# Moving one operand buffer of a float32 two-block transformer kernel by 64 bytes

## The reference

```python
# first block: attention without softmax, then a squared-ReLU MLP
a = rms_norm(x, norm_mix);  q, k, v = split(a @ w_qkv)            # 2048 -> 3 x 2048
A = exp(log_sigmoid(z) + sum of -softplus(z) over later keys)      # z = q k / sqrt(128), masked
h = x + (A @ v) @ w_o
h = h + square(relu(rms_norm(h, norm_mlp) @ w1)) @ w2              # 2048 -> 8192 -> 2048
x = rms_norm(h, final_norm)
# second block: 16 meta tokens are put in front of the 256
hn = rms_norm(concat(meta, x), norm_mix_g)
u, gb, gc, v, ga, gbr = split(hn @ w_in)                           # 2048 -> 6 x 2048
y_a = (trailing means of u over 2, 4, 8, 16 tokens, minus u) @ pool_w * pool_scale
y_b = (gb * causal_conv3(gc * v)) @ conv_out_w
h = x + (sigmoid(ga + b) * y_a + sigmoid(gbr + b) * y_b) @ w_o
h = h + (silu(rms_norm(h) @ w_gate) * (rms_norm(h) @ w_up)) @ w_down   # 2048 -> 5632 -> 2048
out = rms_norm(h, norm_final_g)[the 256 tokens]
```

## Time and profile before

| what | value |
|---|---|
| median of 3 runs | 2618.42 us (2618.08 to 2618.51) |
| the profiled execution | 2618.09 us |
| its span (first to last instruction) | 2616.4 us, granted TensorE clock 0.999 |
| PE busy | 2606.8 us, 16309 products |
| PEld busy | 2351.2 us, 16309 loads |
| DVE, ACT, POOL busy | 1648.6, 1213.5, 142.4 us |
| chain that ended last | PE 99% |
| HBM | 185 GB/s over the span |

### The profile page before, as it was taken

The page is one execution under the profiler, slowest core; times in us unless marked ns, Lnnn a source line. Parts: engine busy times, 40 slices in busy tenths (PEclk is TensorE's granted clock), DMA queues, the critical chain, the costliest instruction groups (busy, mean ns, idle before and its releaser), DMA issues.

```text
span 2616.4 us, 41094 instructions
## 1 busy us (share of the span) xinstructions
PE 2606.8 (100%) x16309; PEld 2351.2 (90%) x16309; DVE 1648.6 (63%) x1406; ACT 1213.5 (46%) x1189; POOL 142.4 (5%) x87
## 2 busy tenths in 40 slices
PE   9999999999999999999999999999999999999998
PEld 9999998888888888899899988888888888888887
DVE  6577666656556556787654776566756555655665
ACT  5455544444444444544533344444544444444444
POOL 0001100000000000000200620000000000000001
PEclk9999999999999999999999999999999999999999
DMA  7554555565565565555555555555555555555563
GB/s 261 183 171 161 163 176 181 190 192 183 188 192 185 186 191 189 181 179 191 182 190 177 180 190 192 184 186 193 187 185 191 191 183 189 192 183 186 193 202 120
DMA packets 243953, 485.24 MB, mean 185 GB/s; under 512 B 7728, under 2 KB 8944, under 8 KB 243696
## 3 DMA queue, kind: packets, MB, share of 16 engines
q1 hardware_dynamic: 243520, 483.12, 56.6%
q10 hardware_dynamic: 320, 0.53, 0.1%
HBM read 481.53 MB, written 2.10 MB: 185 GB/s over the span
## 4 chain that ended last, share of the span: by engine, by line
PE 99%; DVE 0%; DMA 0%; ACT 0%; issue 0%; POOL 0%; SPq 0%; DVEq 0%; ACTq 0%; POOLq 0%
PE ps L1324 46%; PE ps L1330 24%; PE ps L1344 14%; PE ps L1352 7%; PE ps L1312 4%; PE ps L1318 2%; PE ps L1454 0%; PE ps L1366 0%; PE ps L1400 0%; DMA raw<-in_sb_w_qkv_dram 0%; PE ps L1388 0%; PE ps L1459 0%; PE ps L1437 0%; PE ps L1391 0%; DVE wlo L761 0%
## 5 line engine op out<-in xcount | busy, mean ns | idle before, releaser
L761 DVE TENSOR_TENSOR wlo<-raw,whi 128x1024 fp32r<-128x1024 f32 x900 | 1135.3, 1270 | 915.5 <-ACT whi L554 912.6
L554 ACT ACTIVATE whi<-raw 128x1024 fp32r<-128x1024 f32 x900 | 952.4, 1061 | 1314.3 <-PE ps L1330 982.2
L1324 PE MATMUL ps<-b_buf,whi 128*128 128x512 f32 x2688 | 673.3, 392 | 0.0
L1324 PE MATMUL ps<-a_buf,whi 128*128 128x512 f32 x2560 | 645.7, 394 | 0.0
L1324 PEld LDWEIGHTS ps<-b_buf,whi 128*128 128x128 f32 x2688 | 483.5, 189 | 86.5
L1324 PEld LDWEIGHTS ps<-a_buf,whi 128*128 128x128 f32 x2560 | 459.7, 188 | 84.9
L1330 PEld LDWEIGHTS ps<-b_buf,wlo 128*128 128x128 f32 x2688 | 366.7, 190 | 26.2
L1330 PE MATMUL ps<-b_buf,wlo 128*128 128x256 f32 x2688 | 374.8, 282 | 0.0
L1330 PEld LDWEIGHTS ps<-a_buf,wlo 128*128 128x128 f32 x2560 | 346.9, 188 | 27.1
L1330 PE MATMUL ps<-a_buf,wlo 128*128 128x256 f32 x2560 | 354.3, 281 | 0.0
L1344 PE MATMUL ps<-a_buf,whi 128*128 128x258 f32 (+4 forms) x2560 | 330.9, 282 | 0.1
(11 more groups left out here) (190 smaller groups left out, 1052.8 us busy)
## 6 DMA issues: line engine op xcount, KB each, us to landing
raw<-in_mlp_w_dram SPq DMA_DIRECT2D x128, 1024.0 KB, 5.1
raw<-in_w_in_dram SPq DMA_DIRECT2D x96, 1024.0 KB, 5.0
raw<-in_w_gate_up_dram SPq DMA_DIRECT2D x88, 1024.0 KB, 5.0
raw<-in_sb_w_qkv_dram SPq DMA_DIRECT2D x44, 1024.0 KB, 5.1
raw<-in_w_down_dram SPq DMA_DIRECT2D x44, 1024.0 KB, 5.1
raw<-in_sb_w_o_dram SPq DMA_DIRECT2D x16, 1024.0 KB, 5.1
raw<-in_conv_out_w_dram SPq DMA_DIRECT2D x16, 1024.0 KB, 5.0
raw<-in_w_o_dram SPq DMA_DIRECT2D x16, 1024.0 KB, 5.1
```

Source lines behind the costliest of these rows:

```text
L554: act.activation(whi[:, unit_of(n, u)], raw[:, n % RAW, u * UK:(u + 1) * UK, :], ACT.Copy).then_inc(w_hi, 1)
L761: dve.tensor_tensor(wlo[:, s], raw[:, n % RAW, u * UK:(u + 1) * UK, :], cast(whi[:, s]), ALU.subtract).then_inc(w_lo, 1)
L1324: pe.matmul(ps[:, 4 * half + j, :].rearrange("p (a n) -> p a n", a=2), whi[:, s, kt, j * P:(j + 1) * P], buf[:, :, x, tok], start=first an ...
```

## The change

Before `b_buf` is placed, the offset goes up by 64 bytes. `b_buf` and all that follows up to `ms` (`h`, `full`, `U`, `S1`, `S2`, `acc`, `rr`, `rr1`, `ms`, and `x_sq`, which shares `b_buf`'s place) start 64 bytes later. `msum` has no place of its own any more: the sum goes to the first 16 columns of `rr`. Since `msum` took 64 bytes, `vec` and all behind it stay where they were. No instruction is added, removed or moved.

```diff
         a_buf, _ = place("a_buf", [P, 2, NT, TW], F32R)
+        top[0] += 64
         b_buf, b_off = place("b_buf", [P, 2, NT, T], F32R)
@@
-        msum, _ = place("msum", [P, M])
+        msum = rr[:, 0:M]
@@
-                dve.tensor_reduce(msum[:], U[:, 1, 0:NT * M].rearrange("p (t n) -> p n t", n=M), mybir.AxisListType.X,
+                dve.tensor_reduce(msum, U[:, 1, 0:NT * M].rearrange("p (t n) -> p n t", n=M), mybir.AxisListType.X,
@@
-                    pe.matmul(ps[:, 6, 0:M], ones[:], msum[:], start=True, stop=True, skip_group_check=True)
+                    pe.matmul(ps[:, 6, 0:M], ones[:], msum, start=True, stop=True, skip_group_check=True)
```

## The result

The changed kernel took 2604.09 us (median of 5 runs, 2603.82 to 2604.91) against 2618.22 us before: ratio 0.9946, 95% interval 0.9936 to 0.9957, 14.1 us less. The prediction was 2613.9 us with a range of 2607 to 2620.

What follows compares the result with a forecast made beforehand. The prediction took the spacing of TensorE's products, which have no idle time ahead, to bound the kernel. Its terms, -3.5 - 2.3 + 1.3 = -4.5 us, gave a predicted median of 2613.9 us, range 2607 to 2620.

Steps and rivals of the forecast that it cites:

- What bounds the kernel: Whole kernel: products have no idle time ahead, so only their start-to-start spacing can change time beyond a few tenths of a microsecond.
- The 256s with `wlo`: 2688 products of 256 columns on `b_buf`: 119.1 to 117.8 ns each, -3.5 us, bounds -11.0 and +2.4 us.
- The 512s: 2688 products of 512 columns on `b_buf`: 230.0 to 230.5 ns each, +1.3 us, bounds -6.7 and +13.4 us.
- The narrow products: 960 products on `b_buf`, 640 with `whi` and 320 with `wlo`: 120.0 to 117.6 ns each, -2.3 us.
- Attention: 80 products of L1366 and L1376 that read `b_buf`: taken as nothing, at most 0.2 us either way.
- the other operands: Operands of VectorE, ScalarE and GpSimd that move by 64 bytes: taken at zero.
- `msum`: The sum placed in `rr`: no instruction or wait more, zero, not above 0.1 us either way.
- no effect: Product spacing on `b_buf`: the remainder does not matter or 64 bytes aren't enough to leave it; 2618.4 us, 26%.
- The slower one: 512-column products on `b_buf` lose their settled 227.5 ns rhythm and go to 235 ns; +7.6 us, 2626 us, 10%.
- The conflict removed: Weight load and stream collide at the shared remainder; a constant offset gives 227.5 and 115 ns, -22.5 us, 2596 us, 14%.
- The bounds: Whole kernel: the terms' bounds together, -22.5 us (2596) and +15.8 us (2634).

## Why the prediction was wrong

*What bounds the kernel*: right. The gain is in product spacing alone, and no idle time appeared beyond the 0.3 us of one wait.

*The 256s with `wlo`*: this step failed, and is the larger part of the miss. It took `a_buf`'s mean of 117.8 ns for `b_buf` at 64 bytes, -3.5 us; measured 115.7 ns, -9.1 us. The nearest row, the k tile of `a_buf` that stands at 64 bytes, would not have saved it. Its 0.46 us for four products comes from two rounded starts; by the unrounded starts of the same trace they take 0.468 us, 117.0 ns each. That the bound of 115 ns lies near the 115.7 measured was luck. In `a_buf` the distance changes every four products, while in `b_buf` it is constant, and there every second unit runs at 113 ns throughout. Nor is `a_buf`'s mean that of the constant places it walks through: with TensorE alone those give 115.7, 118.5, 114.0 and 119.1 ns, 116.8 on average, and `a_buf`'s rows 118.1. The prediction saw a settled rhythm in the 512s of before and did not ask which one the new place would have for the 256s.

*The 512s*: this term failed as well, by 4.5 us: taken as +1.3 us, measured -3.2 us (229.0 ns). The 227.5 ns rhythm of the second half was lost, as feared, and the halves of a unit are equal, 0.91 to 0.92 us. But the new rhythm serves all eight alike: 226, 229 and 232 ns in turn, by the starts of the trace.

*The narrow products*: -2.3 us taken, -1.8 us measured, right in size.

*Attention, the other operands, `msum`*: at nothing, and nothing it was (everything but `b_buf` moved: 0.9999).

*The rivals*: no effect, 26%, is out. The slower one, 10%, is not what happened at 64 bytes, yet it is real at 128, where the kernel is 4.4 us slower (232.8 ns per 512). The conflict removed, 14%, comes nearest, and my argument against it, that `a_buf` off the remainder is no better, was the error of the whole: a mix of distances says little on one constant distance. The argument also counted modulo 512 bytes; the period is 256, so `a_buf` is off the remainder in three of four k tiles and not in seven of eight. But the mechanism of this rival is not shown either: of the 15 other distances tried in steps of 16 bytes, 12 have slower units than the shared remainder, so it is not a conflict that ends when that is left. The bounds, 2596 to 2634, held the time; the range, cut at the middle of that rival, did not.

What stays open is why the distance matters inside TensorE, and what decides between two rhythms at one place. The first was not tried below whole products, nor without the weight loads. Of the second the traces show that narrow units on `b_buf` change their rhythm only where other products or a wait come between them, never inside an unbroken run; nothing here predicts which one they take.

## What to carry to other kernels

Where products follow one another without idle time, sweep the byte distance between weights and moving operand modulo 256 bytes with TensorE alone: 16 places of 8 units each take under 0.4 ms of one run. The paired units tried in the full kernel came within 0.1% of that price. The narrow ones on `b_buf` did so at 0 and 128 bytes alone, since at 64 and 192 they can take either of two rhythms 4% apart. Don't take a buffer whose rows walk through several distances as the price of a constant one. "Not the same remainder" is no rule: 64 bytes gained 14.1 us, 192 gained 11.8, 128 lost 4.4.

## What the runs showed of the hardware

- The distance of operand and weights counts modulo 256 bytes, and moves a unit of 16 products between 2.757 and 2.833 us (2.8%), TensorE alone, in steps of 16 bytes.
- Off a multiple of 16 bytes it can be worse: at 4 bytes a unit takes 2015.43 - 2012.54 = 2.89 us (238.8 and 122.4 ns), at 12 and at 60 bytes 2.77.

```profile
2012.54 2.07 PE L92 MATMUL ps<-mv,whi 128*128 128x512 f32 x8
2014.45 1.14 PE L106 MATMUL ps<-mv,wlo 128*128 128x256 f32 x8
2015.43 2.08 PE L92 MATMUL ps<-mv,whi 128*128 128x512 f32 x8
```

- One place can have two rhythms: the same narrow products at the same places run at 113 or 118 ns each, at 64 as at 192 bytes, and keep to one until a break.
